# Expert rows turned by VectorE, with TensorE left to the products, in a hybrid decoder layer in fp32

## The reference

```python
def expert_block(args):
    tb, eb = args
    xb = x[tb]                                    # 128 rows of RMSNorm(h), width 1024
    h = jax.nn.silu(xb @ w_gate[eb]) * (xb @ w_up[eb])   # 1024 -> 256
    return h @ w_down[eb]                         # 256 -> 1024
...
y = jnp.zeros((N, D), jnp.float32).at[tok_buf].add(y_buf.reshape(P, D) * gate_buf[:, None])
```

## Time and profile before

| | us |
|---|---|
| median of 3 runs | 2599.76 |
| lowest, highest | 2598.04, 2603.17 |
| profiled execution, whole | 2603.91 |
| its span (first to last instruction) | 2602.2 |
| TensorE busy in the span | 2333.2 |
| VectorE, ScalarE, GpSimd busy | 1027.2, 707.5, 456.6 |

### The profile page before, as it was taken

One profiled execution on the slowest core, in us unless ns is written; L12 is line 12 of the kernel. 1 busy time (PEld: TensorE's weight loads), 2 busy tenths in 40 slices (PEclk: granted clock), 3 DMA queues, 4 the chain that ended last, 5 costly groups with the idle time before them and its releaser, 6 DMA issues. The chain is left out here.

```text
span 2602.2 us, 36339 instructions
## 1 busy us (share of the span) xinstructions
PE 2333.2 (90%) x13208; PEld 1339.2 (51%) x13208; DVE 1027.2 (39%) x1762; ACT 707.5 (27%) x1825; POOL 456.6 (18%) x632
## 2 busy tenths in 40 slices
PE   7999999999968999999999999849999999999940
PEld 3454454533546666666667666524444444444420
DVE  4415234224226554456656656341111211112128
ACT  3203122012025544345444554201111111111112
POOL 1010100100200011200131311212222212212235
PEclk9999999999978999899999999969999999999975
DMA  8041230400373112121122111167999999999967
GB/s 283 26 134 33 57 103 9 131 11 11 97 226 76 56 61 88 52 65 56 56 79 88 56 56 61 60 250 297 367 362 361 363 369 370 361 362 361 354 249 314
DMA packets 165971, 440.35 MB, mean 169 GB/s; under 512 B 36961, under 2 KB 78169, under 8 KB 141225
## 3 DMA queue, kind: packets, MB, share of 16 engines
q1 hardware_dynamic: 139351, 350.38, 37.7%
q0 software_dynamic: 20640, 70.29, 6.8%
q10 hardware_dynamic: 5842, 17.80, 1.8%
HBM read 345.11 MB, written 94.80 MB: 169 GB/s over the span
## 5 line engine op out<-in xcount | busy, mean ns | idle before, releaser
L867 PE MATMUL p_ps<-p_xt,p_w 128*128 128x512 f32 x1088 | 476.7, 597 | 0.5 <-DVE p_xt L698 0.5
L3056 PE MATMUL p_ps<-p_w_arena,p_x_arena 128*128 128x512 f32 x1024 | 446.6, 594 | 0.0
L867 PEld LDWEIGHTS p_ps<-p_xt,p_w 128*128 128x128 f32 x1088 | 205.2, 191 | 255.2 <-issue 250.0
L3056 PEld LDWEIGHTS p_ps<-p_w_arena,p_x_arena 128*128 128x128 f32 x1024 | 195.5, 191 | 245.4 <-issue 245.4
L2426 PE MATMUL p_ps<-p_w_out,p_mixt 128*128 128x512 f32 x544 | 252.5, 609 | 0.0
L3072 PE MATMUL p_ps<-p_w_arena,p_y_arena 128*128 128x512 f32 x512 | 236.0, 604 | 0.0
L2978 DVE SCALAR_TENSOR_TENSOR p_y_arena<-p_y_arena,p_ps 128x256 f32<-128x256 f32 x64 | 27.0, 422 | 459.9 <-ACT p_y_arena L2863 358.2
L2426 PEld LDWEIGHTS p_ps<-p_w_out,p_mixt 128*128 128x128 f32 x544 | 99.6, 193 | 105.8 <-issue 103.7
L876 PE MATMUL p_ps<-p_w,p_xt 128*128 128x144 f32 (+1 forms) x512 | 146.6, 440 | 0.0
L2807 POOL DMA_INDIRECT s_y<-p_y_arena,p_home x66 | 65.0, 985 | 462.3 <-PE p_ps L3043 266.6
L3072 PEld LDWEIGHTS p_ps<-p_w_arena,p_y_arena 128*128 128x128 f32 x512 | 93.1, 192 | 98.2 <-issue 93.0
(11 more groups left out here) (415 smaller groups left out, 3254.1 us busy)
## 6 DMA issues: line engine op xcount, KB each, us to landing
p_w_arena<-in_w_exp_gate SPq DMA_DIRECT2D x64, 1024.0 KB, 7.9
p_w_arena<-in_w_exp_up SPq DMA_DIRECT2D x64, 1024.0 KB, 11.1
p_w_arena<-in_w_exp_down SPq DMA_DIRECT2D x64, 1024.0 KB, 10.6
p_w_arena<-s_y SPq DMA_DIRECT2D x16, 1024.0 KB, 13.3
p_x<-in_x_prompt SPq DMA_DIRECT2D x30, 512.0 KB, 4.8
p_w<-in_w_in SPq DMA_DIRECT2D x4, 2048.0 KB, 15.5
p_spread<-s_roots SPq DMA_DIRECT2D x16, 512.0 KB, 7.1
s_kv<-p_us SPq DMA_DIRECT2D x32, 256.0 KB, 2.3
```

What stands on the lines that cost most here:

```text
L867: ins = mm(ps[:, job % 4, :], w[:, c, at:at + P], xt[s % 2][:, c, :], start=(c == 0), stop=(c == KC - 1))
L3056: t = mm(ps[:, 2 + b, :], xt[b][:, c, :], w_gu[bw][:, :, c, :], start=(c == 0), stop=(c == KC - 1))
```

## The change

- x is no longer turned by TensorE. Its rows are gathered in four indirect transfers of 128 quarter rows (1 KB), so that partition group k (32 partitions) holds quarter k of the rows of four groups of tokens; then one VectorE transpose of 32x32 squares gives all of `xt`. `slots` has four columns a block, spread over the partitions by four small matmuls with a selection matrix `sel`.
- mid is turned by sixteen VectorE transposes of 32 x (2x32), partition group g to group q.
- Absent rows get an index beyond the bound and are to be skipped, in gathers and scatters; the x buffers are cleared once by a memset on GpSimd. One spare row is left.
- TensorE's order is gate/up of block j, down of block j-1, one block at a time; the accumulator of y is doubled. The loops of VectorE and ScalarE follow.
- `gather_listed` fetches the ids in five transfers (one column, and four for the four partition groups) and computes with thirteen small operations.
- `hn` is written without a step, and the router weights are loaded in matching order (pieces of 32 and 256 B a row).
- The number, size and order of the weight transfers are as before, three of 1 MB a block.

```diff
--- before.py
+++ after.py
...
-    c["spare"] = (2 * HOMES + 1 + i)[:, None]
+    spare = np.where(i > 0, float(ABSENT), 2.0 * HOMES + 1)
+    c["spare"] = np.stack([spare, np.where(i % 32 > 0, float(ABSENT), 4.0), i // 32], 1)
...
-                    (w_route[:, :, 0:NG], A["w_router_group"][0].rearrange("(p c) n -> p c n", p=P)),
-                    (w_route[:, :, NG:], A["w_router_expert"][0].rearrange("(p c) n -> p c n", p=P))]
+                    (w_route[:, :, 0:NG], A["w_router_group"][0].rearrange("(c p) n -> p c n", p=P)),
+                    (w_route[:, :, NG:], A["w_router_expert"][0].rearrange("(c p) n -> p c n", p=P))]
...
-                stt(hn[:].rearrange("p c q -> p q c"), h[:].rearrange("p (q c) -> p q c", c=KC), hr[:],
-                    gain[:].rearrange("p (q c) -> p q c", c=KC), ALU.mult, ALU.mult).then_inc(hn_ready.sem, 1)
+                stt(hn[:].rearrange("p c q -> p (c q)"), h[:], hr[:], gain[:], ALU.mult, ALU.mult).then_inc(hn_ready.sem, 1)
...
             def gather(j, b):
-                pool.wait_ge(turned.sem, turned.back(j, R))
+                pool.wait_ge(xt_ready.sem, xt_ready.back(j, R))
                 apart(pool, on["slots_ready"], 1)
-                nc.gpsimd.tensor_copy(slot[b][:], slots[:, bass.ds(j, 1)]).then_inc(slot_ready.sem, 1)
+                nc.gpsimd.tensor_copy(slot[b][:], slots[:, :, bass.ds(j, 1)].rearrange("p g o -> p (g o)")).then_inc(slot_ready.sem, 1)
                 fetch_rows(j, b)
 
             def fetch_rows(j, b):
                 pool.wait_ge(slot_ready.sem, slot_ready.all(j))
+                for g in range(4):
+                    apart(pool, on["slots_ready"], 1)
+                    pool.indirect_dma_start(out=x[b][:, 256 * g:256 * g + 256], out_offset=None,
+                                            in_=S["hn"].rearrange("t (q k) -> (t q) k", q=4),
+                                            in_offset=bass.IndirectOffsetOnAxis(ap=slot[b][:, g:g + 1], axis=0),
+                                            bounds_check=4 * NTOK - 1, oob_is_err=False).then_inc(x_in[b], 16)
...
+            def gather_listed(j, b, arrived):
+                n, ts, tt = b % 2, nc.gpsimd.tensor_scalar, nc.gpsimd.tensor_tensor
+                q = pool.value_load(owner[0:1, bass.ds(2 * (j + (R - NE)) + 1, 1)], min_val=0, max_val=NE * PLACES)
...
-                with nc.allow_non_contiguous_dma(reason="one row to one column"):
-                    pool.dma_start(raw[n][:], S["ids"][bass.ds(q, 1)].rearrange("o c -> c o")).then_inc(raw_in[n], 16)
...
+                with nc.allow_non_contiguous_dma(reason="one row to columns"):
+                    pool.dma_start(raw[n][:, 0:1], S["ids"][bass.ds(q, 1)].rearrange("o c -> c o")).then_inc(raw_in[n], 16)
+                    for k in range(4):
+                        pool.dma_start(raw[n][32 * k:32 * k + 32, 1:5],
+                                       S["ids"][bass.ds(q, 1)].rearrange("o (g b) -> b (o g)", g=4)).then_inc(raw_in[n], 16)
...
+                quad = raw[n][:, 1:5]
+                ts(home_f[:], raw[n][:, 0:1], 0.0, None, ALU.is_equal).then_inc(step_own.sem, 1)
+                ts(none_f[:], quad, 0.0, None, ALU.is_equal).then_inc(step_own.sem, 1)
+                ts(token_f[:], quad, HOMES + 1.0, -4.0 * HOMES, ALU.is_ge, ALU.mult).then_inc(step_own.sem, 1)
+                step(3)
...
+                tt(token_f[:], token_f[:], none_f[:], ALU.add).then_inc(step_own.sem, 1)
+                step(11)
                 nc.gpsimd.tensor_copy(homes[:, bass.ds(j, 1)], home_f[:]).then_inc(homes_own.sem, 1)
+                nc.gpsimd.tensor_copy(slot[b][:], token_f[:]).then_inc(slot_ready.sem, 1)
...
-                                        in_=y[b], in_offset=None).then_inc(y_out[b], 16)
+                                        in_=y[b], in_offset=None, bounds_check=2 * HOMES + P - 1, oob_is_err=False
+                                        ).then_inc(y_out[b], 16)
...
+            nc.gpsimd.memset(x_arena[:, 0:R * D], 0.0).then_inc(on["x_cleared"], 1)
+            pool.wait_ge(on["x_cleared"], 1)
...
-                    gather_listed(i + b + R, b, 8 * (i + (2 * R - NE)) + 16 * (b // 2) + 16)
+                    gather_listed(i + b + R, b, 40 * (i + (2 * R - NE)) + 80 * (b // 2) + 80)
...
+            def evacuate_y(j, b, sent):
+                act.wait_ge(down_done.sem, down_done.all(j))
+                act.wait_ge(y_out[b], sent)
+                nc.scalar.copy(y[b][:, 512:], ps[:, 1 if b else 6, :]).then_inc(y_act.sem, 1)
...
+            def blocks(i, first=0):
+                for n in range(first, R):
+                    gate(i + n, n % 2)
+                    evacuate_y(i + n - 1, (n + 1) % 2, 8 * i + 16 * ((n + 1) // 2))
...
+            dve.wait_ge(on["spread"], 1)
+            nc.vector.tensor_scalar(slots, ps[:, 4, 0:4 * NE].rearrange("p (g e) -> p g e", g=4), spare[:, 2:3], None, ALU.add
+                                    ).then_inc(on["slots_ready"], 1)
...
-                nc.vector.tensor_copy(xt[b][:, 0:4, :], ps[:, 0, :].rearrange("p (c t) -> p c t", c=4)
-                                      ).then_inc(xt_vec.sem, 1)
...
+            def turn_x(j, b, bx, x_count):
+                dve.wait_ge(x_in[bx], x_count)
+                dve.wait_ge(gu_done.sem, gu_done.back(j, 2))
+                nc.vector.transpose(xt[b].rearrange("p c (g r) -> p g c r", g=4), x[bx].rearrange("p (g a c) -> p g c a", g=4, c=KC)
+                                    ).then_inc(xt_ready.sem, 1)
...
+            def turn_mid(j, b):
+                dve.wait_ge(mid_ready.sem, mid_ready.all(j))
+                dve.wait_ge(down_done.sem, down_done.back(j, 2))
+                for q in range(4):
+                    for g in range(4):
+                        t = nc.vector.transpose(midt[b][32 * q:32 * q + 32, :, 32 * g:32 * g + 32],
+                                                mid[b][32 * g:32 * g + 32].rearrange("p (q a c) -> p q c a", q=4, c=FC)[:, q])
+                t.then_inc(midt_ready.sem, 1)
+
+            def blocks(i, first=0):
+                for n in range(first, R):
+                    j, b = i + n, n % 2
+                    gate(j, b)
+                    evacuate_y(j - 1, 1 - b, 8 * i + 16 * ((n + 1) // 2))
+                    turn_mid(j, b)
+                    turn_x(j + 2, b, (n + 2) % R, 16 * i + (64 if n < 2 else 128))
...
+            for g in range(4):
+                t = mm(ps[:, 4, g * NE:(g + 1) * NE], sel[:, g].rearrange("p q b -> p (q b)"), token, start=True, stop=True)
+            t.then_inc(on["spread"], 1)
...
-            def turn(j, b, bx, x_count):
-                pe.wait_ge(x_in[bx], x_count)
-                for a in range(2):
-                    pe.wait_ge(xt_act.sem if a else xt_vec.sem, xt_vec.back(j, 1))
-                    for c in range(4):
-                        t = tr(ps[:, a, c * P:(c + 1) * P], x[bx][:, (4 * a + c) * P:(4 * a + c + 1) * P], ident[:])
-                    t.then_inc(turned.sem, 1)
...
+            def gate_up(j, b, bw, arrived):
+                pe.wait_ge(xt_ready.sem, xt_ready.all(j))
+                pe.wait_ge(mid_ready.sem, mid_ready.back(j, 2))
+                pe.wait_ge(gate_in[bw], arrived)
+                pe.wait_ge(up_in[bw], arrived)
+                for c in range(KC):
+                    t = mm(ps[:, 2 + b, :], xt[b][:, c, :], w_gu[bw][:, :, c, :], start=(c == 0), stop=(c == KC - 1))
+                t.then_inc(gu_done.sem, 1)
+
+            def down(j, b, bw, arrived):
+                pe.wait_ge(midt_ready.sem, midt_ready.all(j))
+                pe.wait_ge(down_in[bw], arrived)
+                for n in two:
+                    pe.wait_ge(y_act.sem if n else y_vec.sem, y_vec.back(j, 2))
+                    for c in range(FC):
+                        t = mm(ps[:, n if b else 5 + n, :], midt[b][:, c, :], w_dn[bw][:, c, n * 512:(n + 1) * 512],
+                               start=(c == 0), stop=(c == FC - 1))
+                    t.then_inc(down_done.sem, 1)
+
+            def blocks(i, first=0):
+                for n in range(first, R):
+                    gate_up(i + n, n % 2, n, 4 * i + 16)
+                    down(i + n - 1, (n + 1) % 2, (n - 1) % R, 4 * i + (16 if n else 0))
...
```

More of the change, by code:

```diff
@@ L2653, in moe @@
         owner = sb("owner", [1, 2 * SPILL + 1], I32)
-        slots, homes = sb("slots", [P, NE], I32), sb("homes", [P, SLOTS], I32)
-        slot = [sb(f"slot{b}", [P, 1], I32) for b in ring]
-        raw = [sb(f"raw{b}", [P, 1]) for b in two]
-        home_f, token_f = sb("home_f", [P, 1]), sb("token_f", [P, 1])
-        spare, minus = sb("spare", [P, 1]), sb("minus", [P, n3])
+        homes = sb("homes", [P, SLOTS], I32)
+        slots = K["lg"][:].rearrange("p t n -> p (t n)")[:, 0:4 * NE].rearrange("p (g e) -> p g e", g=4)
+        sel = cut(work, 9 * D, (4, 4, 32))
+        slot = [sb(f"slot{b}", [P, 4], I32) for b in ring]
+        raw = [sb(f"raw{b}", [P, 5]) for b in two]
```

(51 more changed lines are left out.)

140 lines of the change are left out of this document (36 added, 104 removed).

## The result

Changed kernel: 2613.91 us (median of 6 runs, 2607.19 to 2617.05) against 2599.77 for the kernel before (6 runs beside them): ratio 1.0059, 95% interval 1.0041 to 1.0077. It is slower by 0.6%; 2617 was forecast. The profiled execution took 2617.05 us, its span is 2615.3 (before: 2602.2).

The account below looks back on a forecast made before the run. TensorE was taken to pace the even stretch, DMA close behind, and GpSimd the stage's ends. 2603.91 + 18.8 - 1 = 2621.7, less the 4.15 by which the profiled run exceeded the median: 2617 us, range 2588 to 2655.

Parts of the forecast that it names:

- 1: Without TensorE's turns a block takes 10.30 us instead of 11.52; VectorE's work, about 7.5 us a block, stays hidden.
- 2: DMA in the even stretch: 9.5 to 9.8 us a block, under 10.30, so taken as adding 0.
- 3: GpSimd in the even stretch: 7.9 to 9.3 us a block, under 10.30; gap g between gathers taken as 0.31 us.
- 4: Stage start: ids scatters begin at about 1766 and take 41 us; TensorE starts block 4 at 1818 after waiting 27 us.
- step 5: End of the even stretch: block 57 begins at 2363.9, the first list transfer 3 us later at 2366.9; 46 us won.
- step 6: GpSimd's second loop: 17.8 us a turn plus 27 us of load; last scatter at 2535.1, 18.8 us later than before.
- 7: Earlier phases: normed rows without a step -1 to -3 us, router weights 0 to +4 us; -1 taken in all.
- B: Rival, chance 0.30: GpSimd's issues at the stage's end are cheaper; a 15.5 us turn gives no change, 14.4 gives 2590.
- C: Rival, chance 0.08: absent rows still occupy DMA, which bounds the even stretch at 11.0 us a block; 37 us more, 2654.
- D: Rival, chance 0.08: GpSimd can't keep pace in the even stretch, 10.8 us a block; 27 us there and at the end, 2670.
- E: Rival, chance 0.03: the list transfers at the end are served one by one, 75 us, giving 2692.
- F: Rival, chance 0.04: VectorE is the bound at 11.0 us a block, with twice the price of small turns; 2654.

Follow-up runs that it names:

- a_absent_read: The changed kernel, but places without a token gather row 0 instead of being skipped (blocks 0 to 59): 2603.10 us, ratio 1.0025 to the kernel before.
- a_ids_late: The changed kernel, with the eight ids scatters issued one in each of the first eight blocks: 2575.56 us, ratio 0.9910 to the kernel before.
- a_no_chain: The changed kernel, but a y scatter no longer waits until the one before it has landed: 2598.65 us, ratio 1.0001 to the kernel before.
- a_plain_end: The changed kernel, with blocks 60 to 63 gathered like the others and no second loop: 2528.75 us, ratio 0.9725 to the kernel before.
- a_mended: The changed kernel with the edits of a_plain_end and a_ids_late together: 2499.74 us, ratio 0.9627 to the kernel before.
- a_one_list: The changed kernel with one list transfer a turn in place of five: 2591.66 us, ratio 0.9983 to the kernel before.
- a_mid_more: a_ids_late with the sixteen small VectorE turns made twice, once into memory nobody reads: 2645.57 us, ratio 1.0188 to the kernel before.

## Why the prediction was right

The sign and the reason held: TensorE's gain in the middle, and more than all of it given back by GpSimd at the ends. The size, 2617 against 2613.91, came out by two large errors of opposite sign. Step by step:

1. TensorE, 10.30 us a block: exact. VectorE's turns: 2.03 us (taken 2.0) and 0.25 in a row (0.22); its block without waits is 11.45 - 4.0 = 7.4 us (7.5).
2. DMA 0.94 x 10.3 = 9.7 us a block (9.5 to 9.8), hidden. The price of the absent rows was near: in `a_absent_read` q0's share rose by 6.8 points, 0.70 us a block, for 0.8. But 0.5 us was not all the room there was: with them moved nothing got slower.
3. GpSimd: g is 0.30 us (0.31); its block takes 8.15 us when it catches up (7.9).
4. The start: ids scatters from 1762.65, over 38.6 us later (1766, 41); block 4 at 1810.87 (1818), after a wait of 22.3 us (27). Each term was taken a little long.
5. **The step that missed.** Block 57 began at 2358.77 (2363.9; block 4, at a lower clock, took 2.0 us over 10.30), but the first list transfer came 14.0 us behind it, not 3: 2372.78 for 2366.9. I had looked at the scatters for their issue alone. Their landings had been 8.8 us at the median in the kernel before, under the block of 11.52; with a block of 10.30 the chain of landings and issues has the pace of TensorE and never makes up what the start cost. `a_ids_late` and `a_no_chain` price it at 10 to 12 us.
6. The turn of the second loop: 17.1 us (17.8). The four further list issues follow without a gap, 2.23 for 3.12 us; the wait 2.68 (2.52), the small operations 4.16 (4.00), the gathers 5.1 (5.33) were right. The load: 154.69 - 7 x 17.1 - 15.9 = 19.1 us (27). So the end, 154.7 for 168.2, was 13.5 us cheaper than thought and paid for step 5: the last scatter came at 2527.47, not 2535.1.
7. Earlier phases: the first slot copy came 1.35 us earlier (taken: 1 earlier by these phases, 2.5 later by the slots). One profile can't tell that from chance, but all can: it starts at 1729.65 to 1737.46 in the eleven with the change and at 1737.48 to 1740.80 in the three without, 5.9 us earlier on the mean. One part of it is seen: the write of `hn`, the same operation without the step, takes 1.28 us for 2.05 at the median, 17 times. So the term was taken too small. The last stage took 1.9 more.

The errors of 4 and 6, to the good, and of 5, to the bad, cancel in part. The 3 us of the total are luck, and so in part are the 0.6%: the 11 us of step 5 and the 13.5 of step 6 are each as large as the 14 us that the change costs. What isn't luck is the mechanism, a gain in the middle and a longer chain of GpSimd behind it, which `a_plain_end`, `a_ids_late` and `a_mended` show.

Rivals. B fell by its own point: the turn is 17.1 us, over 15.5, and the gathers of a block that holds nothing cost 1.20, 1.03, 1.00 and 0.99 us like the others. C's 2654 was wrong in its consequence for the gathers, by `a_absent_read` (the absent rows of its scatters were still left out; no run moves those too). D: 8.15 us instead of 10.8. E: one wait of 2.68 us serves all five transfers; four issues of 0.56 us in each turn, 17 us in all by `a_one_list`, and not 75. The Trainium skill (DMA: Bandwidth & Descriptors, Rules for kernel authors) warns of many small transfers; the runs agree in the sign, and show the price as time of the engine that issues them, not of the DMA. F: its price was right in kind; `a_mid_more` shows it at 11.45 us a block.

## What to carry to other kernels

When a pipeline's middle gets faster, price its ends at the new number of instructions first: here 1.2 us a block x 64 was won, and four list turns, four empty ones and eight waited scatters took it back, though the empty turns could go, the scatters could be spread, and the lists could be fetched a turn ahead. Compare every chain that waits for its own landing (here one y scatter at a time, 9.4 + 0.9 us) with the new pace: a chain just at the pace keeps any lag it gets. And judge a change with the ends mended in both kernels (0.9627 against 0.9920, both without the blocks of an expert's further tokens) as well as by the total (1.0059).
